# The opening of a diffusion-transformer step: filter decays, modulation and input, reordered

## The reference

```python
shift, scale, gate = jnp.split(silu(c) @ w_mod[l] + b_mod[l], 3, axis=-1)
h = x * (1 + scale) + shift
proj = h @ w_in[l]          # 3*512 Hyena | q, k, v | MLA | paths | merge gates
filt = hyena_filters(...)   # below
y_hy = hyena(hy_in, ...)    # short convolution, two long convolutions with filt
... # differential attention, latent attention, gates, w_branch, w_out, layer norm
```

```python
def hyena_filters(n_tok, w1, b1, w2, b2, w3, sin_freq, log_decay):
    feats = [t_lin, cos(ang), -sin(ang)]                     # (n_tok, 33)
    hid = sin(sf[0] * (feats @ w1 + b1))
    hid = sin(sf[1] * (hid @ w2 + b2))                       # (n_tok, 64)
    h = hid @ w3
    return h * exp(-t_lin[:, None] * exp(log_decay))         # (n_tok, 2, 2, 512)
```

## Time and profile before

| what | value |
|---|---|
| median of three runs | 1870.74 us |
| the profiled execution's own time | 1869.32 us |
| its span | 1867.3 us |
| TensorE busy | 1777.1 us, 95% |
| VectorE busy | 1153.7 us, 62% |
| ScalarE busy | 681.9 us, 37% |
| GpSimd busy | 477.5 us, 26% |
| DMA | 150.04 MB, 80 GB/s over the span |

### The profile page before, as it was taken

The page is one execution under the profiler, slowest core; times in us unless marked ns, Lnnn a source line. Parts: engine busy times, 40 slices in busy tenths (PEclk is TensorE's granted clock), DMA queues, the critical chain, the costliest instruction groups (busy, mean ns, idle before and its releaser), DMA issues.

```text
span 1867.3 us, 28231 instructions
## 1 busy us (share of the span) xinstructions
PE 1777.1 (95%) x11464; PEld 1588.5 (85%) x11464; DVE 1153.7 (62%) x1620; ACT 681.9 (37%) x1174; POOL 477.5 (26%) x230
## 2 busy tenths in 40 slices
PE   5899999999999999999889999999999999999996
PEld 2888799878888888999877969998888888889996
DVE  5598894454464544576977989925544644435745
ACT  3424312444244544322273342224433454442122
POOL 0100033221241211467200000422223412125651
PEclk9999999999999999999999999999999999999998
DMA  9111122111211111354521112221112111115431
GB/s 357 46 57 35 34 91 74 51 51 55 68 35 56 45 39 50 136 192 136 229 91 35 57 34 70 78 68 40 55 57 68 37 46 53 43 46 184 139 113 62
DMA packets 50448, 150.04 MB, mean 80 GB/s; under 512 B 9674, under 2 KB 13898, under 8 KB 49552
## 3 DMA queue, kind: packets, MB, share of 16 engines
q1 hardware_dynamic: 46720, 134.09, 21.7%
q10 hardware_dynamic: 3600, 14.16, 2.2%
HBM read 141.63 MB, written 6.59 MB: 79 GB/s over the span
## 4 chain that ended last, share of the span: by engine, by line
PE 70%; DVE 17%; issue 5%; ACT 4%; DMA 2%; POOL 2%; SPq 0%; ACTq 0%; DVEq 0%; POOLq 0%
PE PS L835 16%; PE PS L836 15%; PE PS L840 15%; PE PS L907 4%; PE PS L896 3%; PE PS L1092 2%; PE PS L938 2%; PE PS L941 2%; PE PS L920 2%; DVE Wl L1577 1%; POOL Wl L2018 1%; DVE work L1550 1%; DVE work L1549 1%; DVE MG L1822 1%; ACT Wh L1215 1%
## 5 line engine op out<-in xcount | busy, mean ns | idle before, releaser
L2018 POOL TENSOR_TENSOR Wl<-W,Wh 128x1024 fp32r<-128x1024 f32 (+3 forms) x178 | 372.5, 2093 | 1227.5 <-ACT Wh L1215 1188.2
L835 PE MATMUL PS<-Hh,Wh 128*128 128x320 f32 x2048 | 613.2, 314 | 13.2 <-ACT Wh L1215 8.9
L836 PE MATMUL PS<-Hl,Wh 128*128 128x320 f32 x2048 | 605.1, 310 | 0.0
L835 PEld LDWEIGHTS PS<-Hh,Wh 128*128 128x128 f32 x2048 | 386.6, 189 | 36.7 <-issue 24.7
L836 PEld LDWEIGHTS PS<-Hl,Wh 128*128 128x128 f32 x2048 | 386.8, 189 | 0.2
L840 PE MATMUL PS<-Hh,Wl 128*128 128x320 f32 x2048 | 321.4, 309 | 0.6 <-POOL Wl L2018 0.6
L840 PEld LDWEIGHTS PS<-Hh,Wl 128*128 128x128 f32 x2048 | 305.5, 188 | 1.0 <-POOL Wl L2018 1.0
L1556 DVE TENSOR_REDUCE st<-PS 128x1 f32<-128x640 f32 (+1 forms) x160 | 114.9, 718 | 277.0 <-PE PS L920 155.9
L1215 ACT ACTIVATE work<-PS 128x640 f32<-128x640 f32 (+8 forms) x276 | 169.7, 624 | 227.2 <-PE PS L840 78.9
L1215 ACT ACTIVATE Wh<-W 128x1024 fp32r<-128x1024 f32 (+3 forms) x210 | 188.4, 900 | 64.0 <-PE PS L840 26.5
L1372 ACT ACTIVATE th<-PS 128x640 f32<-128x640 f32 x64 | 45.0, 703 | 341.2 <-PE PS L840 341.2
(11 more groups left out here) (253 smaller groups left out, 2592.8 us busy)
## 6 DMA issues: line engine op xcount, KB each, us to landing
W<-in_w_in SPq DMA_DIRECT2D x132, 512.0 KB, 3.5
W<-in_w_branch SPq DMA_DIRECT2D x48, 256.0 KB, 2.7
work<-in_w_mod_rows ACTq DMA_DIRECT2D x23, 512.0 KB, 4.1
pmod_w<-in_w_mod SPq DMA_DIRECT2D x8, 1024.0 KB, 11.2
W<-in_w_out SPq DMA_DIRECT2D x16, 512.0 KB, 4.5
work<-in_x_sample SPq DMA_DIRECT2D x2, 2048.0 KB
late_modulation_w<-in_w_mod_rows SPq DMA_DIRECT2D x5, 512.0 KB, 6.6
x_mid<-work SPq DMA_DIRECT2D x1, 2560.0 KB, 8.5
```

What stands on the lines that cost most here:

```text
L835: pe.matmul(out, Wh[:, b, kk, :], xh[:, kk, t], start=kk == 0, stop=False)
L836: pe.matmul(out, Wh[:, b, kk, :], xl[:, kk, t], start=False, stop=False)
L2018: return pool.tensor_tensor(out, in_, high.bitcast(f32), ALU.subtract)
```

## The change

Six things are changed. They touch the opening of layer 0, except that `project_two` serves both layers.

1. log_decay is loaded as one row of 8 KB (`expld[0:1]`); new steps `ldec` 0 and 1 spread it over 128 partitions by products with a row of ones, four fp32 products of 1x512 in all, and ScalarE takes the exponential out of PSUM in two operations of 128x1024.
2. The order becomes ffn 0, lam, ldec 0, 1, ffn 1, pmrow 0, filt 0, pmrow 1, filt 1, pmod 0, pmrow 2, pmod 1, filt 2, pmrow 3, pmod 2, 3, then the stream with filt 3 behind two 2 and filt 4 behind two 4, conv 0 to 3, and all five fdft.
3. The queue's order becomes: small ones and w3, the row, w_mod blocks 0 to 7 in a row, the two weight tiles, x in two column halves with a semaphore each, and then `fwd` and `fwdc`.
4. `ht` 0 and `ht` 4 wait each for its half of x.
5. In `ht` 1, ScalarE makes h 1 without waiting for h 0, and then copies the high halves of both; VectorE makes the two weight low parts in `ht` 1 and 2, behind Hl 0 and Hl 1.
6. In `project_two` the products with the low weight part lag by two steps (`LOW_LAG`), and `two` 7 makes up for three.

```diff
+LOW_LAG = 2
...
-        s = [("lam", 0)] + f[:6] + rows[:2] + f[6:7] + p[:2] + rows[2:3] + p[2:3] + f[7:10] + rows[3:] + p[3:]
-        s += start_steps([], {})
-        s += [("conv", c) for c in range(CT)] + f[10:]
+        s = f[:1] + [("lam", 0), ("ldec", 0), ("ldec", 1)] + f[1:2] + rows[:1] + f[2:3] + rows[1:2] + f[3:4] + p[:1]
+        s += rows[2:3] + p[1:2] + f[4:5] + rows[3:] + p[2:]
+        s += start_steps([], {2: f[5:6], 4: f[6:7]})
+        s += [("conv", c) for c in range(CT)] + f[7:]
...
+                    if l == 0 and dst is expld_in:
+                        dst, src = dst[0:1], A["hy_log_decay"][0:1]
                     sp.dma_start(dst, src).then_inc(HERE[part], 16)
...
             layer_tables(0, 1)
-            for g in range(NP):
-                first_modulation(g)
-            layer_tables(0, 2)
-            load_x(0)
-            for g in range(NP, KD):
+            for g in range(KD):
                 first_modulation(g)
             weight(0)
             weight(1)
+            load_x(0, ((slice(0, D // 2), x_here), (slice(D // 2, D), x_rest)))
+            layer_tables(0, 2)
...
+                lows = range(kk - LOW_LAG, kk - LOW_LAG + 1) if kk < KD - 1 else range(kk - LOW_LAG, KD)
...
-                    if kk == 0:
+                for i in range(2):
+                    outs = ...
+                    if kk == LOW_LAG:
                         pe.wait_ge(*after("w_lo", l, i + 1))
-                    for out, t in outs:
-                        last = pe.matmul(out, Wl[:, i, kk, :], Hh[:, kk, t], start=False, stop=kk == KD - 1)
+                    for k in lows:
+                        ...
+                        for out, t in outs:
+                            last = pe.matmul(out, Wl[:, i, k, :], Hh[:, k, t], start=False, stop=k == KD - 1)
...
+                    elif kind == "ldec":
+                        pe.wait_ge(*freed(l, kind, i))
+                        ps = slot(l, kind, i)
+                        if i == 0:
+                            pe.wait_ge(filter_here, 16 * N_FILTER)
+                        for b in range(2):
+                            last = pe.matmul(ps[:, HY * b:HY * b + HY], ones[0:1, :], expld[0:1, i, b, :], start=True, stop=True)
+                        last.then_inc(full_of(l, kind, i), 1)
...
+                    elif kind == "ldec":
+                        if i == 0:
+                            act.wait_ge(*after("lam_sum", 0, 1))
+                            act.activation(lamc[:, 4:6], lamc[:, 4:6], ACT.Exp).then_inc(sems["lam_exp"], 1)
+                        act.wait_ge(*filled(l, kind, i))
+                        act.activation(expld[:, i].rearrange("p a b -> p (a b)"), slot(l, kind, i)[:, :], ACT.Exp).then_inc(sems["ld_read"], 1)
...
                             if i == 1:
-                                act.wait_ge(*after("h_f32", l, 1))
+                                act.wait_ge(*after("ss_ready", l, 2 * KD))
...
+                            if i == 1:
+                                act.wait_ge(*after("h_f32", l, 1))
+                                copy(Hh[:, 0, :], th[:, 0]).then_inc(sems["h_hi"], 1)
...
-                            act.wait_ge(filter_here, 16 * N_FILTER)
-                            link(act.activation(expld, expld, ACT.Exp))
+                            act.wait_ge(*after("ld_read", 0, 2))
...
-                        if l == 0 and i < 2:
-                            low_part(l, i)
                         for c in [i - 1] * (i > 0) + [i] * (i == KD - 1):
                             dve.wait_ge(*after("h_hi", l, c + 1))
                             TT(Hl[:, c, :], th[:, c % 2], Hh[:, c, :].bitcast(f32), ALU.subtract).then_inc(sems["h_lo"], 1)
                             dve.wait_ge(*own("h_lo"))
+                        if l == 0 and i in (1, 2):
+                            low_part(l, i - 1)
```

More of the change, by code:

```diff
@@ L265 @@
     "pmrow": lambda i: [("row_ready", i + 1)],
+    "ldec": lambda i: [("ld_read", i + 1)],
     "ht": lambda i: [("h_act" if i % 2 else "h_f32", i // 2 + 1)],
@@ L708, in _, with load_x @@
             sp.dma_start(crow, A["c_rows"]).then_inc(consts_here, 16)
-            def load_x(l):
+            def load_x(l, parts=((slice(0, D), x_here),)):
                 if l == 0:
-                    sp.dma_start(X[:, 0:4, :], A["x_sample"][0].rearrange("(t p) d -> p t d", p=128))\
-                      .then_inc(x_here, 16)
-                    sp.dma_start(X[:, 4, :], A["x_prompt"][0]).then_inc(x_here, 16)
+                    for c, here in parts:
+                        sp.dma_start(X[:, 0:4, c], A["x_sample"][0, :, c].rearrange("(t p) d -> p t d", p=128))\
+                          .then_inc(here, 16)
+                        sp.dma_start(X[:, 4, c], A["x_prompt"][0, :, c]).then_inc(here, 16)
                 else:
@@ L854, in project_two @@
                         pe.matmul(out, Wh[:, i, kk, :], Hl[:, kk, t], start=False, stop=False)
-                    if kk == 0:
+                for i in range(2):
+                    outs = [(slot(l, "two", 0, i)[:, 512 * a:512 * a + HALF], slice(HALF * a, HALF * a + HALF)) for a in range(2)]
+                    if kk == LOW_LAG:
                         pe.wait_ge(*after("w_lo", l, i + 1))
-                    for out, t in outs:
-                        last = pe.matmul(out, Wl[:, i, kk, :], Hh[:, kk, t], start=False, stop=kk == KD - 1)
+                    for k in lows:
+                        if k < 0:
+                            continue
+                        for out, t in outs:
+                            last = pe.matmul(out, Wl[:, i, k, :], Hh[:, k, t], start=False, stop=k == KD - 1)
                     if kk == KD - 1:
@@ L965, in _ @@
                         ps = slot(l, kind, i)
-                        if i == 0:
-                            if l:
-                                pe.wait_ge(*after("x_ready", l - 1, 5))
-                            else:
-                                pe.wait_ge(x_here, 32)
+                        if i == 0 and l:
+                            pe.wait_ge(*after("x_ready", l - 1, 5))
+                        elif i in (0, KD // 2) and not l:
+                            pe.wait_ge(x_rest if i else x_here, 32)
                         for t in range(NT):
@@ L1327, in _ @@
                         if l == 0 and i == 0:
-                            act.wait_ge(*after("lam_sum", 0, 1))
-                            act.activation(lamc[:, 4:6], lamc[:, 4:6], ACT.Exp).then_inc(sems["lam_exp"], 1)
-                            act.wait_ge(filter_here, 16 * N_FILTER)
-                            link(act.activation(expld, expld, ACT.Exp))
+                            act.wait_ge(*after("ld_read", 0, 2))
                             act.activation(decay, expld[:, :, 0, :], ACT.Exp, scale=negt[:, 0:1]).then_inc(sems["decay_ready"], 1)
@@ L1686, in _ @@
                         a, k = rr[:, 0], rr[:, 1]
+                        if kind == "ffn" and i == 0:
+                            dve.wait_ge(small_here, 16 * N_SMALL)
                         if i:
```

9 lines of the change are left out of this document (6 added, 3 removed).

## The result

| kernel | median of 20 runs | lowest, highest | profiled execution (span) |
|---|---|---|---|
| before | 1869.05 us | 1864.46, 1871.73 | 1869.32 (1867.3) |
| after | 1873.03 us | 1868.33, 1876.60 | 1875.88 (1873.9) |

The ratio after to before is 1.0022, 95% interval 1.0015 to 1.0030. The change made the kernel 0.22% slower, some 4 us, and the interval reaches across the 0.2% that the prediction put between "slower" and "no change". The three runs of before that stood ahead of the prediction had a median 1.7 us above the one of 20.

A forecast was written before the change was run, and what follows sets the result against it. The queue was taken to decide up to about 40 us, TensorE from 50 to 94. Terms -7.2 + 6.9 + 0.3 = 0.0 us, so no change that can be told: 1870.9 us, range 1866.5 to 1876.

The forecast's parts named there:

- rival (a): Opening and stream: half clock delays block 7's issue to 27.3, hole 2.6 us, stream slow until two 5; +4.9 us, chance 0.21.
- S: Mark in layer 0's opening: when x's first columns can be transposed; forecast at 36.0 us.
- E: Mark: first copy out of layer 0's finished stream, at 70.08 before; forecast at 62.9, 7.2 us earlier.
- D: Mark: VectorE's first product of the data's transforms, 99.10 before; data transforms forecast to start within 2 us of 96.3.
- Part 1: Opening loads: 4344 KB less ahead of block 7, which could land at 29.4; x's first half at 35.2, smaller pieces 0.1 us.
- Part 2: Opening: decay row's products take some 6 us, ffn 1 starts 3.6 us later; hole before block 7 0.7 us, S = 36.0.
- Part 3: Layer 0's stream: first h to E 25.8 us, 5.8 longer, as ht 7 waits for filt 3; E 7.2 us earlier.
- Part 4: Behind conv 3: fdft 0 to 2 add their 6.87 us in full, their VectorE work costing 0.
- rival (b): Opening to conv 2: no hole, VectorE's chain 0.5 shorter, clock stays up behind the stream; 3.3 to 4 us faster, chance 0.10.
- Part 5: Layer 1's stream: the lag costs +0.3 us, bounds -0.3 and +1.2.
- The rule against it: Stream's start: skill says transposes don't count as busy, so clock stays 1.2 GHz through two 0 to 2; forecast assumed otherwise.
- (c): Behind conv 3: the moved transforms vanish in idle time, so the earlier start survives; -7 us, 1864, chance 0.04.

The follow-up runs named there:

- e11: The changed kernel once more, unaltered, in the same call as its variants; ratio to before 1.0026.
- e1: The changed kernel with w_mod blocks 5 to 7 in memory of their own, the inverse tables' load waiting for pmrow 3 instead; ratio to before 0.9998.
- e8: The changed kernel with four fp32 products of 128x512, results overwritten, in TensorE's idle time before the first transposes; ratio to before 1.0007.
- e10: The changed kernel with only the two weight low parts put back in their old place, ht 0 and 1, the lag kept; ratio to before 1.0008.
- e2: The changed kernel with filt 3 and 4 also ahead of the stream, so all five filters are; ratio to before 0.9990.
- e3: The changed kernel with LOW_LAG = 0 in the old order of products and the low parts made in ht 0 and 1 again; ratio to before 1.0003.
- e5: e3 with Hh 0 copied ahead of h 1, as in the kernel before; ratio to before 1.0005.
- e7: e1, e2 and e5 together, plus fdft 0 to 2 ahead of two 0 and their tables loaded between the halves of x; ratio to before 0.9984.
- e12: e9 with the filters' steps ahead of the modulation steps (pmrow 1 to 3) where possible; 1864.83 us, ratio to before 0.9977.
- e9: e7 with the decay row's products cut by filter order, the second half spread behind conv 3; 1863.01 us, ratio to before 0.9969.

## Why the prediction was nearly right

The predicted time, 1870.9, lies 2.1 us under the median, and the range held it. The difference says more, since it is free of the choice of the runs of before: forecast 0.2 us, measured some 4. It is the size of rival (a) (+4.9), and the reason is half of rival (a)'s. That the time itself came out within 0.1% is luck in part: the median of before that it starts from lay 1.7 us too high, which hid half of the miss. Step by step:

| term, us | forecast | after | e11 |
|---|---|---|---|
| S | 36.0 | 39.39 | 38.17 |
| S to the first h | 1.1 | 1.41 | 1.41 |
| first h to E | 25.8 | 27.64 | 26.13 |
| D - E, over before's | 6.87 | 6.84 | 6.84 |
| D, over before's | -0.3 | 5.20 | 2.47 |

Of the prediction's own signs the wait of ht 7, the 12 us piece of transforms and ffn 1 ahead of 16 us came true. Block 7's issue (27.22 for 24), no gap in the DMA near 25 us, and the start of the data's transforms within 2 us of where they were (5.0 us later in after, 2.5 in e11) did not; the first h (34 to 40) and E (60 to 67) lie inside in e11 and outside in after.

**Part 1, right.** Without a hole the first half of x was to land at 35.3; e1, which has none, starts at 34.67. The smaller pieces cost nothing that can be seen.

**Part 2, the products, right; the hole, mis-sized: this is the term that failed.** ffn 1's product was forecast at 14.3 and came at 14.75; four products took 7.16 us. But I counted one hole, for block 7, and took 0.7 of its 0 to 2.6 us. There are two. The hole for block 7 differs between executions of the same loads: in after pmrow 1 ran at half clock (3.64 us), block 7 was issued at 27.22 and not at 24, and the hole is 2.4 us; in e11 pmrow 1 took 3.27 and the hole is 1.6 (244 GB/s in the same window); in e8 and e10 it took 1.95, and there is none (395 and 399 GB/s). The other hole is in all four (192 to 229 GB/s from 18 to 22 us), and I had not seen it: blocks 5 and 6 wait for pmrow 0, which ended at 19.65. I had followed only block 7's release; before, blocks 5 and 6 stood behind tables and x in the queue, and their wait cost nothing; the change took this cover away, 2.0 us. e1, in which no block waits for a buffer, has neither hole, and its S is 4.7 us earlier and its time that of before: this shows the cause of x's lateness. SyncE's issues in after (start us, length, count) show both releases:

```profile
19.71 0.88 SPq L708 DMA_DIRECT2D pmod_w<-in_w_mod  x2
27.22 0.37 SPq L708 DMA_DIRECT2D pmod_w<-in_w_mod  x1
```

S was 39.39, and 38.17 in e11, for 36.0. Where pmrow 1 ran at full clock it was 37.47 (e8) and 37.17 (e10), 2.8 and 2.5 us behind e1.

**Part 3, right within 0.3 in e11, 1.8 short in after.** ht 7's transposes were forecast 16.7 us behind the first h; they stand at 57.54 - 40.80 = 16.74, in e11 too. From there 9.1 were forecast, e11 has 9.39, after 10.90 with the clock fallen. The half clock until two 5 that rival (a) feared did not come. What I did not see is that 2.8 of these us are the lag and the low parts' place: I had them in the sum as given, not as parts that the change could be without.

**Part 4, right.** 6.87 us forecast; D - E grew by 6.84 in after and in every kernel that leaves the transforms behind conv 3. The two exceptions, 34.3 us in e2 and e10, are those in which conv 2 ran at full clock (rival (b) below).

**Part 5, small, and right by luck.** +0.3 forecast, +0.5 measured up to the copy out of layer 1's stream, inside its bounds. But its parts are a loss of 0.8 by h 1's place on ScalarE, which I had taken to be a matter of layer 0 alone, and a gain of 0.35 by the lag, which alone was forecast to lose 0.3.

**The balance.** E came 1.64 us earlier in after and 4.37 in e11, for 7.2; with 6.84 for the transforms, D is 5.2 and 2.5 later. These offsets are carried unchanged to layer 1: ScalarE's pass ahead of its stream starts at 949.49 in before, at 954.62 in after and at 951.98 in e11 (5.1 and 2.5 later), and the copy out of the stream is 5.6 and 3.0 later. Behind it the clock decides. From the second copy to the third, conv 2's products, layer 1 takes 10.86 us in before (977.44 to 988.30) and 9.38 in after (983.08 to 992.46) and in e11; the granted clock in before is 0.58 and 0.56 from 978 to 982 us, and 1.00 in the other two.

```profile
988.30 0.83 ACT L1215 ACTIVATE raw<-PS 128x320 f32<-128x320 f32 x3 [7.12 <-PE PS L840]
992.46 0.83 ACT L1233 ACTIVATE raw<-PS 128x320 f32<-128x320 f32 x3 [5.62 <-PE PS L845]
```

The first row is before's, the second after's: 4.2 us apart, and 1.5 in e11. By the end they are 6.6 and 3.7 apart, the spans' difference, and 1.5 of this came back by a fall of the clock that before doesn't have (0.77 and 0.50 from 1426 to 1430 us in after, 1.00 in before). So time did move behind 100 us, in pieces of about 1.5 us by the clock, against the last of the prediction's signs. What makes the clock fall in one of these places and not in the other stays open. Over the table's thirteen kernels, D and the median differ from before's by the same amount only within some 3 us: e10's D is 1.8 us ahead of before's and its median 1.3 behind. A mark of one execution can thus explain a stretch, and not a median to the microsecond.

**The rule against it.** In after the clock was at 0.50 when the transposes began at 39.39 and stayed there through them and through two 0, to 47.8, unlike in layer 1 of before, where transposes alone brought it back; in e3 and e11 all 20 transposes ran at half speed (4.50 and 4.46 us), and the products behind them at full, from 43.87 and 43.31; in e5 and e10 the 20 took 3.95 and 4.04 us, so that the last of them ran at full speed. In e11 it fell once more, from 46 to 49. The Trainium skill ("TensorE: Matmul & The Clock Gate", Part 4: PE-mode transpose) says that a transpose doesn't count as busy for the gate in the way a product does: after fits it, layer 1 of before, e5 and e10 don't, and e3 and e11 leave it open. Little of the time hangs on it here, since VectorE sets the pace of that stretch: after and e11 both have 14.01 us from the first h to filt 3, and e1 and e8, at full clock from the start, 13.5.

**The rivals.** (a) was right in the hole and wrong in its other half: the stream was to stay at half clock until two 5, 3 us more; the clock did stay low at first, for 0.5 us, and fell again behind filt 3, for 1.5. (b)'s piece exists: from the second copy out of the stream to the third, conv 2's products, it takes 9.01 to 9.03 us in before, after and eight others and 7.48 or 7.49 in e2, e7, e10 and e12. The wait for Wh ahead of it is 1.94 us in all of them, so its length does not decide; what does is open. (c) fell: behind conv 3 the transforms cost their full length, and even where TensorE waits (e7, e9) most of it.

## What to carry to other kernels

When loads are reordered so that the queue holds only what waits for buffers, follow every waiting load to its release, and not only the last: a wait that costs nothing now is covered by the loads in front of it. Work that fills a wait has a price the day it is moved; here it was better to move it into the next wait (TensorE's, ahead of two 0) than behind the stream, by 2.6 us of D, and its work on the other engines moved with it. And prices of single edits don't add up where the filters, the modulation and x end within a few us of one another: each edit that removes the last one uncovers the next.

## What the runs showed of the hardware

- Early in an execution TensorE can work at half speed while the granted clock reads 1.00. In after it reads 1.00 up to 36 us, and the same 64 products took 3.64 us at 16.01 and at 23.52, and 1.95 at 28.66; in before they took 1.95 at 24.74, in e8 at 22.84. When half speed ends differs, so up to there the speed has to be read from durations.
- A fp32 product with one row of weights costs what one with 128 costs: four of 512 columns in 7.16 us at half speed, 1.79 each, where the filter transforms' rate gives 1.72. At full clock, behind conv 3 in e9, two of them took 1.98 us and the two transform products ahead of them, with 128 rows, 1.88.
- A wait of TensorE of about 2 us can cost 1.5 us more behind it, by the clock, or nothing: ahead of ht 7, waits of 1.2 to 1.4 us left it up and 2.10 brought it down; at the 1.94 us for Wh behind the stream both occur. In e12 it fell with no wait at all.
- The transposes of x's first half began between 37.2 and 39.4 us in executions of kernels whose loads are the same (after, e2, e3, e5, e8, e10, e11), and this goes through to E.
